# A decoder-layer kernel: rotary key tile in two weight passes, conditioning shared out anew between TensorE, GpSimd, VectorE and ScalarE

## The chip, the cores and the metric

The kernel runs on one core of a Trainium2 chip. Times are device microseconds of one launch, from the first to the last instruction of the core. Lower is better. TensorE multiplies, VectorE (DVE in the rows) and ScalarE (ACT) do the elementwise work out of SBUF and PSUM, GpSimd (POOL) does elementwise work out of SBUF alone, and SyncE (SP) issues most of the transfers.

## The reference

One hybrid decoder layer over 1024 tokens and 1024 features, in float32:

```python
mod = jax.nn.silu(c) @ w_ada[l] + b_ada[l]
shift, scale, gate = jnp.split(mod[:, None, :], 3, axis=-1)
h = rmsnorm(x, g_pre[l]) * (1.0 + scale) + shift
proj = h @ w_in[l]
(c_q, c_kv, k_pe, gate_mla, q_ret, k_ret, v_ret, gate_ret,
 merge_mla, merge_ret) = jnp.split(proj, pts, axis=-1)
y_mla = mla_branch(c_q, c_kv, k_pe, positions, g_q[l], w_q_up[l], g_kv[l], w_kv_up[l])
y_ret = retention_branch(q_ret, k_ret, v_ret, positions, g_ret[l]) * jax.nn.silu(gate_ret)
...
x = x + gate * (merged @ w_out[l])
return rmsnorm(x, g_final)
```

What matters here is the start. `c` is one vector of 1024 numbers; shift and scale are 2048 sums of 1024 products each ("the conditioning"). `h` is the normed input, scaled and shifted per feature. `k_pe` is 64 of the columns of `proj`; it is one rotary key shared by all eight heads, and inside `mla_branch` it is turned by the rotary angles, where component i and component i+32 are mixed.

## The kernel before, in words

**Precision.** Every float32 product is made of three passes over TensorE in the format fp32r: an operand is split into a rounded high part (`_hi`, written by ScalarE, `split_weight` for weights, `high` for h) and the remainder (`_lo`, written by VectorE, `lower_weight` and `low`), and the passes are hi·hi, hi·lo and lo·hi. `w_raw`, `w_hi` and `w_lo` are rings of three weight tiles of 128 columns.

**The start, in order.** x arrives, is normed on VectorE and turned on TensorE (`x_t`, features on partitions). The conditioning weights `ada` come in four quarters q, each with shift and scale for two feature tiles of h. In a quarter the 1024 inputs stand as eight tiles k of 128 partitions: GpSimd multiplies tile 0 by silu(c) (line 976, into `stage`), VectorE adds tiles 1 to 7 on (`weigh`, lines 1501 and 1508, into `ada_sum`), and TensorE then sums over the partitions with a column of ones (`weigh_sums`, line 1951). In quarter 0 TensorE multiplies tile 0 itself (line 1984), with silu(c) as the moving column. VectorE adds bias and gain (`modulation`, lines 1516 to 1521), and signals `mod_ready`.

**h.** From `mod`, ScalarE makes the rounded `h_hi` (line 1090) and GpSimd the full `h_full` (line 984), both 128x1024 for each feature tile; VectorE subtracts them into `h_lo` (line 1528). VectorE's queue for a quarter is: `weigh(q+1)`, `low(2q)`, `low(2q+1)`, `modulation(q+1)`.

**First three tiles.** r = 0 is the rotary key tile: its 128 columns are the 64 of `k_pe` twice. r = 1 and 2 are the first latent tiles. TensorE does them feature tile by feature tile as h comes: `early_hi` (lines 1968 and 1969: w_hi·h_hi and w_lo·h_hi for two halves of 512 tokens each) and `early_lo` (line 1976: w_hi·h_lo). In front of `early_lo(2q)` stands `weigh_sums(q+1)`. Feature tiles 6 and 7 are done tile by tile of r. Then r = 3, 4, 5 run in full (`products`, lines 2005 to 2007), 48 matmuls each.

**The rotary key and the sums of h.** After `low(7)` VectorE goes through: the MLA angles (`angles(1)`, lines 1445 to 1451), `lower_weight(3)`, the retention angles (`angles(0)`), `lower_weight(4)` and `(5)`; then k_pe times cosine (line 1554), the swapped halves times sine (1555), their sum (1558); then four sums or differences over parts of h (1561 to 1569), their low parts (1572), and the low part of the first "form" (1579), a combination of weights for the stage that follows: 25 pairs of weight tiles in a seven-product scheme (`pair_products`, lines 2090 to 2093). ScalarE meanwhile evicts `k_pe` from PSUM (line 1198), and SyncE copies it with its blocks of 32 rows swapped into `swap` (line 668), after VectorE's first instruction of the retention angles (`table` 8). GpSimd starts the sums of pair 0 when `roped` is 5.

Everything behind (the 25 pairs, up-projections, attention with the value projection filled in, retention, merge, output) is the same in both kernels.

Of the kernel before, what the change touches and what calls it, by code (L numbers as in the profile page):

```python
# [21 lines left out]
P = 128  # L22
# [87 lines left out]
ADA_STEPS = KD - 1  # L110
# [10 lines left out]
class Layer:  # L121
# [3 lines left out]
    def __init__(self, nc, sem, a, t, d, out, pools):  # L125
# [113 lines left out]
        self.out_stage = [self.stage[:, 0, :], self.stage[:, 1, :], late_stage[:, 0, :], late_stage[:, 1, :]]  # L239
        self.v_stage = [nc.alloc_sbuf_tensor_at("v_stage_0", [P, 2, HALF], F32R, offset=stage_at),  # L240
# [285 lines left out]
    def lower_weight(self, dve, r):  # L526
        if r >= R_END:
            return
        dve.wait_ge(*((self.w_hi_ready, r) if r else (self.first_w_hi_ready, 1)))
        self.nc.vector.tensor_tensor(self.lo_place(r), self.raw_place(r), self.hi_place(r).bitcast(F32), ALU.subtract)\  # L530
            .then_inc(self.w_lo_ready, 1)
# [88 lines left out]

    def form_bank(self, pair, n):

        return (5 * pair + n + 3) % 8
# [23 lines left out]
    def sync(self, sp):  # L647
# [26 lines left out]
        sp.wait_ge(self.roped, 5)  # L674
# [290 lines left out]
    def gpsimd(self, pool):  # L965
        nc, rot = self.nc, self.rot
        nc.gpsimd.memset(self.t["ones"][:, :], 1.0).then_inc(self.ones_ready, 1)

        def weigh(q):

            part = self.stage[:, q % 2, :].rearrange("p (s n) -> p s n", s=2)
            pool.wait_ge(self.ada_loaded[q], 16)
            if q >= 2:
                pool.wait_ge(self.ada_step, ADA_STEPS * (q - 1))
            pool.wait_ge(self.silu_ready, 1)
            nc.gpsimd.tensor_scalar(part, self.ada[:, q, :, 0, :], self.silu_c[:, 0:1], None, ALU.mult)                .then_inc(self.ada_part, 1)

        def full(k):
            c = 4 * (k // 2) + k % 2
            pool.wait_ge(self.mod_ready, 2 * (k // 2) + 2)  # L980
            if k == 0:
                pool.wait_ge(self.x_early, X_EARLY)
                pool.wait_ge(self.x_late, 2 * KD - X_EARLY)
            nc.gpsimd.tensor_scalar(self.h_tile(k), self.x_t[:, k, :], self.mod[:, c + 2:c + 3],
                                    self.mod[:, c:c + 1], ALU.mult, ALU.add).then_inc(self.h_full_ready, 1)

        for q in range(4):
            if q < 3:
                weigh(q + 1)
            full(2 * q)  # L990
            full(2 * q + 1)
        for pair in range(PAIRS):
            a11, a12, total, a21 = (self.form_source(FORMS * pair + n) for n in (0, 4, 1, 3))
            a22 = self.form_source(FORMS * pair + 5)
            made = SUMS + FORMS * pair
            pool.wait_ge(self.pair_loaded[pair % 2], 16 * (pair // 2 + 1))
            if pair:
                pool.wait_ge(self.form_lo, made - FORMS + 2)
            else:
                pool.wait_ge(self.roped, 5)  # L1000
# [59 lines left out]
    def scalar(self, act):  # L1060
# [31 lines left out]

        self.split_weight(act, 1)
# [4 lines left out]
        for k in range(1, KD):  # L1098
            high(k)
        for r in range(R_UP):  # L1100
# [375 lines left out]
    def vector(self, dve):  # L1476
# [16 lines left out]
        def weigh(q):  # L1493

            out = self.ada_sum[:, q, :, :]
            dve.wait_ge(self.ada_loaded[q], 16)
            dve.wait_ge(self.ada_part, q) if q else dve.wait_ge(self.silu_ready, 1)
            for k in range(1, KD):
                before = out
                if k == 1 and q == 0:  # L1500
                    nc.vector.tensor_scalar(out, self.ada[:, 0, :, 1, :], self.silu_c[:, 1:2], None, ALU.mult)\
                        .then_inc(self.ada_step, 1)
                    continue
                if k == 1:
                    before = self.stage[:, q % 2, :].rearrange("p (s n) -> p s n", s=2)
                else:
                    dve.wait_ge(self.ada_step, ADA_STEPS * q + k - 1)
# [24 lines left out]
        dve.wait_ge(self.w_loaded[0], 16)  # L1532
        nc.vector.tensor_copy(self.w_hi[:, 0, :], self.w_raw[:, 0, :]).then_inc(self.first_w_hi_ready, 1)
# [23 lines left out]
        dve.wait_ge(self.roped, 2)  # L1557
# [4 lines left out]
        dve.wait_ge(self.roped, 4)  # L1562
# [364 lines left out]
    def tensor(self, pe):  # L1927
# [18 lines left out]
        def weigh_sums(q):  # L1946
            pe.wait_ge(self.ada_step, ADA_STEPS * (q + 1))
# [11 lines left out]
        def early_hi(k, tiles):  # L1959

            pe.wait_ge(self.h_hi_ready, k + 1)
            for r in tiles:
                if k == 0:
                    pe.wait_ge(self.w_lo_ready, r + 1)
                for half in range(2):
# [3 lines left out]
                    nc.tensor.matmul(out, w_lo[:, r, cut], h_hi[:, k, tok], start=False, stop=False)  # L1969
# [599 lines left out]
```

## Time and profile before

| what | value |
|---|---|
| median of 3 runs | 1615.43 us |
| the runs | 1615.06, 1615.43, 1618.31 us |
| span of the profiled execution | 1616.2 us (the page gives no other time for it) |
| TensorE, busy share of the span | 97% |
| VectorE, ScalarE, GpSimd | 59%, 37%, 20% |
| mean granted TensorE clock | 0.994 of full |

The busy shares are means over stages with different limits. In a row of the timeline the columns are start, busy time, engine, line, operation, tiles and count, and in brackets the idle time in front of it and who ended it. Matmuls of 512 columns are pipelined, so a row shows 0.39 us where the next one starts 0.227 us later. A row that ends in x2 or more is several instructions merged.

### The profile page before, as it was taken

The numbers are of one execution on the slowest core, as the hardware profiler recorded it, in microseconds if no ns is written. First come the engines' busy times: TensorE is split into PE (matmuls) and PEld (weight loads), VectorE is DVE, ScalarE is ACT, GpSimd is POOL, SyncE is SP. The second block draws the span as 40 slices with busy tenths as digits, with TensorE's granted clock in tenths as the row PEclk, the third lists the DMA queues.
The fourth block names the chain that finished last, engine by engine and source line by source line (L and its number), as shares of the span: only waits on it lengthen the run. The fifth ranks groups of instructions, "written<-read, shape, count | busy, mean of one in ns | idle before, by whom it ended". The sixth has DMA issues, their size and how long they took to land. (4 is left out here: it accounts for less than half of the span.)

```text
span 1616.2 us, 20288 instructions
## 1 busy us (share of the span) xinstructions
PE 1568.4 (97%) x7568; PEld 1308.9 (81%) x7568; DVE 959.4 (59%) x1626; ACT 605.1 (37%) x1057; POOL 322.0 (20%) x280
## 2 busy tenths in 40 slices
PE   5999999999999999999999999899999999999998
PEld 4778888888888888798888888787688888888886
DVE  6984444444444457752566665567987775647544
ACT  5444333333333343342343433334544443213111
POOL 2232223322322200200000000015655530000000
PEclk9999999999999999999999999999999999999999
DMA  9132332223323334799265554447977767345422
GB/s 385 38 130 105 111 112 110 107 109 115 120 104 111 95 97 164 301 414 322 82 209 170 181 184 164 179 137 260 323 235 228 250 204 281 115 137 183 143 105 78
DMA packets 142225, 278.70 MB, mean 172 GB/s; under 512 B 11056, under 2 KB 83632, under 8 KB 133552
## 3 DMA queue, kind: packets, MB, share of 16 engines
q1 hardware_dynamic: 125488, 245.09, 43.6%
q10 hardware_dynamic: 12032, 15.54, 2.9%
q0 software_dynamic: 4608, 16.78, 2.7%
q8 instruction: 61, 1.00, 0.2%
q14 instruction: 36, 0.29, 0.1%
HBM read 182.47 MB, written 94.37 MB: 171 GB/s over the span
## 5 line engine op out<-in xcount | busy, mean ns | idle before, releaser
L1579 DVE TENSOR_TENSOR w_form<-w_pair,w_form 128x512 fp32r<-128x512 f32 x150 | 116.3, 776 | 127.2 <-ACT w_form L1211 125.6
L1211 ACT ACTIVATE w_form<-w_pair 128x512 fp32r<-128x512 f32 x150 | 94.6, 632 | 245.3 <-PE p_banks L2093 237.2
L2090 PE MATMUL p_banks<-h_hi,w_form 128*128 128x512 f32 x300 | 116.8, 389 | 1.1 <-DVE w_form L1579 1.1
L2093 PE MATMUL p_banks<-h_hi,w_form 128*128 128x512 f32 x300 | 116.7, 389 | 0.0
L2092 PE MATMUL p_banks<-h_lo,w_form 128*128 128x512 f32 x300 | 116.7, 389 | 0.0
L1283 ACT ACTIVATE prob<-p_banks,neg_max 128x128 f32<-128x128 f32 (+3 forms) x64 | 47.5, 742 | 182.9 <-DVE neg_max L1693 182.9
L524 ACT ACTIVATE w_hi<-w_raw 128x1024 fp32r<-128x1024 f32 (+2 forms) x69 | 59.5, 866 | 144.9 <-PE p_banks L2348 96.2
L2348 PE MATMUL p_banks<-y_hi,w_lo 128*128 128x512 f32 x256 | 99.6, 389 | 0.0
L2347 PE MATMUL p_banks<-y_lo,w_hi 128*128 128x512 f32 x256 | 99.6, 389 | 0.0
L2346 PE MATMUL p_banks<-y_hi,w_hi 128*128 128x512 f32 x256 | 99.6, 389 | 0.0
L1055 POOL DMA_DIRECT2D v_ret<-v_stage x32 | 17.7, 554 | 410.1 <-DVE v_stage L1670 410.0
L530 DVE TENSOR_TENSOR w_lo<-w_raw,w_hi 128x1024 fp32r<-128x1024 f32 (+3 forms) x70 | 72.0, 1033 | 35.4 <-ACT w_hi L524 34.7
L2132 PE MATMUL p_banks<-w_hi,h_hi 128*128 128x512 f32 x192 | 78.8, 410 | 0.6 <-DVE w_lo L530 0.6
L1008 POOL TENSOR_TENSOR w_pair<-w_pair 128x512 f32<-128x512 f32 x25 | 32.5, 1299 | 232.2 <-DVE w_form L1579 232.2
L2090 PE MATMUL p_banks<-h_sum_hi,w_form 128*128 128x512 f32 x200 | 77.9, 389 | 0.0
L2093 PE MATMUL p_banks<-h_sum_hi,w_form 128*128 128x512 f32 x200 | 77.8, 389 | 0.0
L2092 PE MATMUL p_banks<-h_sum_lo,w_form 128*128 128x512 f32 x200 | 77.8, 389 | 0.0
L2090 PE MATMUL p_banks<-h_forms,w_form 128*128 128x512 f32 x200 | 77.8, 389 | 0.0
L2092 PE MATMUL p_banks<-h_forms,w_form 128*128 128x512 f32 x200 | 77.8, 389 | 0.0
L2093 PE MATMUL p_banks<-h_forms,w_form 128*128 128x512 f32 x200 | 77.8, 389 | 0.0
L2132 PE MATMUL p_banks<-w_lo,h_hi 128*128 128x512 f32 x192 | 76.6, 399 | 0.0
L2132 PE MATMUL p_banks<-w_hi,h_lo 128*128 128x512 f32 x192 | 76.5, 398 | 0.0
(316 smaller groups left out, 4302.7 us busy)
## 6 DMA issues: line engine op xcount, KB each, us to landing
w_pair<-in_w_pairs SPq DMA_DIRECT2D x25, 1024.0 KB, 4.9
w_raw<-in_w_dense SPq DMA_DIRECT2D x45, 512.0 KB, 4.7
v_ret<-v_stage POOLq DMA_DIRECT2D x32, 512.0 KB, 3.4
v_chunk<-v_ret SPq DMA_DIRECT2D x32, 512.0 KB, 3.7
merge_t<-act_t SPq DMA_DIRECT2D x48, 256.0 KB, 3.4
act_t<-stage SPq DMA_DIRECT2D x40, 256.0 KB, 2.0
act_t<-stage_late SPq DMA_DIRECT2D x40, 256.0 KB, 2.0
ada<-in_w_ada SPq DMA_DIRECT2D x4, 2048.0 KB, 23.9
```

The source lines that it names most:

```text
L524: self.nc.scalar.activation(self.hi_place(r), self.raw_place(r), ACT.Copy).then_inc(self.w_hi_ready, 1)
L530: self.nc.vector.tensor_tensor(self.lo_place(r), self.raw_place(r), self.hi_place(r).bitcast(F32), ALU.subtract)\
L1211: self.nc.scalar.activation(self.form[f % FORM_SLOTS][:, 0, :], self.form_source(f), ACT.Copy).then_inc(self.form_hi, 1)
L1283: nc.scalar.activation(self.prob[:, g % 2, 0:width], p[:, 6:8, :].rearrange("p a n -> p (a n)")[:, 0:width], ACT.Exp, bias=self.neg_max[:, ...
L1579: nc.vector.tensor_tensor(self.form[f % FORM_SLOTS][:, 1, :], self.form_source(f), self.form[f % FORM_SLOTS][:, 0, :].bitcast(F32), ALU.su ...
L2090: self.nc.tensor.matmul(out, w_hi[:, cut], x_hi[:, q, :], start=fresh and q == 0, stop=False, skip_group_check=True)
L2092: self.nc.tensor.matmul(out, w_hi[:, cut], x_lo[:, q, :], start=False, stop=False, skip_group_check=True)
L2093: last = self.nc.tensor.matmul(out, w_lo[:, cut], x_hi[:, q, :], start=False, stop=q == KD // 2 - 1, skip_group_check=True)
L2132: ins = self.nc.tensor.matmul(self.p[:, FILL_BANKS[unit % 3], :], h[:, k, tok], w[:, cut], start=(k == 0 and kind == 0), stop=(k == KD - 1 ...
L2346: self.nc.tensor.matmul(out, self.w_hi[:, slot, cut], self.y_hi[y][:, tok], start=(k == 0), stop=False)
L2347: self.nc.tensor.matmul(out, self.w_hi[:, slot, cut], self.y_lo[y][:, tok], start=False, stop=False)
L2348: return self.nc.tensor.matmul(out, self.w_lo[:, slot, cut], self.y_hi[y][:, tok], start=False, stop=(k == KD - 1))
```

## The change

1. **Rotary key tile in two passes.** `lower_weight(0)` writes the low part of the 64 columns into the second 64 columns of `w_hi` of tile 0, instead of a `w_lo` tile. `early_hi` leaves out the w_lo pass for r = 0. Rows 0 to 63 of the product then hold hi·h, rows 64 to 127 lo·h. SyncE copies the halves, exchanged, into a new tile `k_other` (in the place of `stage`), and VectorE adds it to `k_pe` behind the retention angles. `roped` counts one more from there on.
2. **Conditioning.** In quarter 0 TensorE multiplies tiles 0, 1 and 2 (`PE_K`), VectorE 3 to 7. In quarters 1 to 3 GpSimd multiplies tiles 0 and 1 in place and adds them (`POOL_K`), VectorE takes 2 to 7.
3. **h_full** goes from GpSimd to ScalarE, behind both `high` of its quarter; the first `w_hi` goes from VectorE to ScalarE.

```diff
@@ lower_weight
+        if r == 0:
+            second, raw = (w.rearrange("p (k n) -> p k n", n=P)[:, :, ROPE:P] for w in (self.hi_place(0), self.raw_place(0)))
+            self.nc.vector.tensor_tensor(second, raw, second.bitcast(F32), ALU.subtract).then_inc(self.w_lo_ready, 1)
+            return
@@ sync
         sp.wait_ge(self.evicted, 2)
+        for half in range(2):
+            sp.dma_start(self.k_other[ROPE * half:ROPE * (half + 1), :], self.k_pe[ROPE * (1 - half):ROPE * (2 - half), :])\
+                .then_inc(self.swapped, 16)
         sp.wait_ge(self.table, 8)
+        sp.wait_ge(self.roped, 1)
         for q in range(4):
             sp.dma_start(self.swap[32 * q:32 * q + 32, :], self.k_pe[32 * (q ^ 1):32 * (q ^ 1) + 32, :])\
@@ gpsimd
+            for k, part in enumerate((first, second)):
+                nc.gpsimd.tensor_scalar(part, part, self.silu_c[:, k:k + 1], None, ALU.mult).then_inc(self.ada_part, 1)
+            pool.wait_ge(self.ada_part, 3 * q - 1)
+            nc.gpsimd.tensor_tensor(first, first, second, ALU.add).then_inc(self.ada_part, 1)
@@ scalar
+        def full(k):
+            c = 4 * (k // 2) + k % 2
+            nc.scalar.activation(self.h_tile(k), self.x_t[:, k, :], ACT.Identity,
+                                 scale=self.mod[:, c + 2:c + 3], bias=self.mod[:, c:c + 1]).then_inc(self.h_full_ready, 1)
+        act.wait_ge(self.w_loaded[0], 16)
+        nc.scalar.activation(self.w_hi[:, 0, :], self.w_raw[:, 0, :], ACT.Copy).then_inc(self.first_w_hi_ready, 1)
...
-        for k in range(1, KD):
+        high(1)
+        full(0)
+        full(1)
+        for k in range(2, KD, 2):
             high(k)
+            high(k + 1)
+            full(k)
+            full(k + 1)
@@ vector
         weigh(0)
-        dve.wait_ge(self.w_loaded[0], 16)
-        nc.vector.tensor_copy(self.w_hi[:, 0, :], self.w_raw[:, 0, :]).then_inc(self.first_w_hi_ready, 1)
         modulation(0)
...
             if r == RING:
                 self.angles(dve, 0)
+                dve.wait_ge(self.swapped, 32)
+                nc.vector.tensor_tensor(self.k_pe[:, :], self.k_pe[:, :], self.k_other[:, :], ALU.add).then_inc(self.roped, 1)
         dve.wait_ge(self.sines, 2)
-        dve.wait_ge(self.swapped, 64)
+        dve.wait_ge(self.swapped, 96)
@@ tensor
                     nc.tensor.matmul(out, w_hi[:, r, cut], h_hi[:, k, tok], start=(k == 0), stop=False)
-                    nc.tensor.matmul(out, w_lo[:, r, cut], h_hi[:, k, tok], start=False, stop=False)
+                    if r:
+                        nc.tensor.matmul(out, w_lo[:, r, cut], h_hi[:, k, tok], start=False, stop=False)
...
-            nc.tensor.matmul(p[:, 6, 16 + c:17 + c], self.ada[:, 0, c // 2, 0, c % 2 * P:(c % 2 + 1) * P],
-                             self.silu_c[:, 0:1], start=True, stop=True)
+            for k in range(PE_K):
+                nc.tensor.matmul(p[:, 6, 16 + c:17 + c], self.ada[:, 0, c // 2, k, c % 2 * P:(c % 2 + 1) * P],
+                                 self.silu_c[:, k:k + 1], start=(k == 0), stop=(k == PE_K - 1))
```

VectorE's queue from the end of the MLA angles to the first sum over h, before:

```order
L1451 TENSOR_SCALAR angle_mla<-angle_mla 128x1024
L530 TENSOR_TENSOR w_lo<-w_raw,w_hi 128x1024
L1445 TENSOR_SCALAR angle_ret<-positions,consts 128x1024
L1446 TENSOR_SCALAR turns_ret<-angle_ret 128x1024
L1447 TENSOR_SCALAR turns_ret<-turns_ret 128x1024
L1449 SCALAR_TENSOR_TENSOR angle_ret<-turns_ret,angle_ret 128x1024 x3
L1451 TENSOR_SCALAR angle_ret<-angle_ret 128x1024
L530 TENSOR_TENSOR w_lo<-w_raw,w_hi 128x1024 x2
L1554 TENSOR_TENSOR k_pe<-k_pe,cos_mla 128x1024
```

The same stretch of VectorE's queue in the changed kernel:

```order
L1461 TENSOR_SCALAR angle_ret<-positions,consts 128x1024
L1462 TENSOR_SCALAR turns_ret<-angle_ret 128x1024
L1463 TENSOR_SCALAR turns_ret<-turns_ret 128x1024
L1465 SCALAR_TENSOR_TENSOR angle_ret<-turns_ret,angle_ret 128x1024 x3
L1467 TENSOR_SCALAR angle_ret<-angle_ret 128x1024
L1568 TENSOR_TENSOR k_pe<-k_pe,k_pe_other_half 128x1024
L536 TENSOR_TENSOR w_lo<-w_raw,w_hi 128x1024 x2
L1571 TENSOR_TENSOR k_pe<-k_pe,cos_mla 128x1024
```

The addition of the exchanged halves stands between the retention angles and the two low parts of weights.

ScalarE's queue in the conditioning, from the end of the copies of `x_t` to the eviction of the rotary key tile, before:

```order
L524 ACTIVATE w_hi<-w_raw 128x1024
L1090 ACTIVATE h_hi<-x_t,mod 128x1024
L524 ACTIVATE w_hi<-w_raw 128x1024
L1090 ACTIVATE h_hi<-x_t,mod 128x1024 x7
L1198 ACTIVATE k_pe<-p_banks 128x512 x2
```

And in the changed kernel:

```order
L1102 ACTIVATE w_hi<-w_raw 128x1024
L526 ACTIVATE w_hi<-w_raw 128x1024
L1093 ACTIVATE h_hi<-x_t,mod 128x1024
L526 ACTIVATE w_hi<-w_raw 128x1024
L1093 ACTIVATE h_hi<-x_t,mod 128x1024
L1098 ACTIVATE h_full<-x_t,mod 128x1024 x2
L1093 ACTIVATE h_hi<-x_t,mod 128x1024 x2
L1098 ACTIVATE h_full<-x_t,mod 128x1024 x2
```

ScalarE now makes two full tiles behind two rounded ones in each quarter.

## Rows read from the trace of the kernel before

**Rows 1.** The page, section 1: busy time of each engine

```profile
PE 1568.4 (97%) x7568; PEld 1308.9 (81%) x7568; DVE 959.4 (59%) x1626; ACT 605.1 (37%) x1057; POOL 322.0 (20%) x280
```

**Rows 2.** Timeline, TensorE at the two hand-overs behind the first tiles

```profile
74.23 0.50 PE L2005 MATMUL p_banks<-h_hi,w_hi 128*128 128x512 f32 x1 [1.55 <-DVE w_lo L530]
...
106.77 0.39 PE L2007 MATMUL p_banks<-h_hi,w_lo 128*128 128x512 f32 x1
108.28 0.50 PE L2090 MATMUL p_banks<-h_hi,w_form 128*128 128x512 f32 x1 [1.12 <-DVE w_form L1579]
```

**Rows 3.** Timeline, VectorE from the MLA angles to the first form

```profile
66.33 0.75 DVE L1445 TENSOR_SCALAR angle_mla<-positions,consts 128x1024 f32<-128x1024 int32 x1
...
72.95 1.22 DVE L530 TENSOR_TENSOR w_lo<-w_raw,w_hi 128x1024 fp32r<-128x1024 f32 x1
74.09 0.75 DVE L1445 TENSOR_SCALAR angle_ret<-positions,consts 128x1024 f32<-128x1024 int32 x1
...
80.72 2.35 DVE L530 TENSOR_TENSOR w_lo<-w_raw,w_hi 128x1024 fp32r<-128x1024 f32 x2
82.99 1.22 DVE L1554 TENSOR_TENSOR k_pe<-k_pe,cos_mla 128x1024 f32<-128x1024 f32 x1
...
107.55 0.68 DVE L1579 TENSOR_TENSOR w_form<-w_pair,w_form 128x512 fp32r<-128x512 f32 x1
```

**Rows 4.** The tile k_pe_swap: SyncE's four copies, and their landing

```profile
L668 SPq DMA_DIRECT2D k_pe_swap<-k_pe x4: 582/594/618, 74.9 to 76.8; - x4
...
DMA to landing us min/median/max: 2.3/2.3/2.4
```

**Rows 5.** Timeline, VectorE: single operations of the conditioning, alone and beside GpSimd

```profile
32.82 0.75 DVE L1508 SCALAR_TENSOR_TENSOR ada_sum<-ada,silu_c,stage 128x512 f32<-128x512 f32 x1
42.49 1.59 DVE L1508 SCALAR_TENSOR_TENSOR ada_sum<-ada,silu_c,ada_sum 128x512 f32<-128x512 f32 x1
49.08 2.36 DVE L1528 TENSOR_TENSOR h_lo<-h_full,h_hi 128x1024 fp32r<-128x1024 f32 x2
61.47 0.16 DVE L1521 SCALAR_TENSOR_TENSOR mod<-mod,cols 128x2 f32<-128x2 f32 x1
```

**Rows 6.** Timeline, GpSimd: products of the conditioning, full tiles of h, a sum

```profile
27.26 1.63 POOL L976 TENSOR_SCALAR stage<-ada,silu_c 128x512 f32<-128x512 f32 x1 [26.44 <-DMA ada<-in_w_ada]
34.45 1.98 POOL L976 TENSOR_SCALAR stage<-ada,silu_c 128x512 f32<-128x512 f32 x1
61.73 1.20 POOL L984 TENSOR_SCALAR h_full<-x_t,mod 128x1024 f32<-128x1024 f32 x1 [7.11 <-DVE mod L1521]
90.15 3.21 POOL L1001 TENSOR_TENSOR w_sum<-w_pair 128x512 f32<-128x512 f32 x1 [25.00 <-DVE k_rope_made L1563]
...
115.17 1.28 POOL L1001 TENSOR_TENSOR w_sum<-w_pair 128x512 f32<-128x512 f32 x1
```

**Rows 7.** The tile ada: its transfers' landing in us from issue

```profile
L656 SPq DMA_DIRECT2D ada<-in_w_ada x4: 436/895/1202, 4.1 to 8.5; - x4
...
DMA to landing us min/median/max: 16.9/23.9/30.5
```

**Rows 8.** Timeline, TensorE and ScalarE in the conditioning: partition sums, products, h_hi

```profile
26.91 1.05 PE L1951 MATMUL p_banks<-ones,ada_sum 128*128 128x1 f32 x8 [2.37 <-DVE ada_sum L1508]
...
43.29 0.39 PE L1968 MATMUL p_banks<-h_hi,w_hi 128*128 128x512 f32 x1
43.52 0.39 PE L1969 MATMUL p_banks<-h_hi,w_lo 128*128 128x512 f32 x1
...
61.67 2.38 ACT L1090 ACTIVATE h_hi<-x_t,mod 128x1024 fp32r<-128x1024 f32 x2 [7.55 <-DVE mod L1521]
```

**Rows 9.** Windows: busy time of each engine, then granted TensorE clock, DMA share, GB/s

```profile
24.50:26.90 2.40, 0.04 (x1) 0.00 (x0) 2.30 (x4) 0.98 (x2) 0.00 (x0) 1.00 0.91 377
26.90:28.00 1.10, 1.05 (x8) 0.97 (x8) 0.56 (x2) 0.00 (x0) 0.74 (x1) 1.00 1.24 518
28.00:30.10 2.10, 0.00 (x0) 0.00 (x0) 2.03 (x5) 1.43 (x2) 2.10 (x2) 0.75 1.04 445
30.10:34.00 3.90, 3.83 (x9) 3.12 (x10) 3.80 (x4) 1.89 (x2) 3.90 (x2) 0.50 0.98 416
35.80:38.40 2.60, 2.60 (x12) 1.89 (x10) 2.49 (x4) 0.00 (x0) 0.63 (x1) 0.99 0.93 371
```

More of the change, by code:

```diff
@@ L109 @@
 X_EARLY, X_BANKS = 5, [0, 1, 2, 3, 4, 5, 7]
-ADA_STEPS = KD - 1
+POOL_K = 2
+PE_K = 3
 CHUNKS = [1, 1, 1, 1, 2, 2, 2, 2]
@@ L239, in __init__ @@
         self.out_stage = [self.stage[:, 0, :], self.stage[:, 1, :], late_stage[:, 0, :], late_stage[:, 1, :]]
+        self.k_other = nc.alloc_sbuf_tensor_at("k_pe_other_half", [P, S], F32, offset=stage_at)
         self.v_stage = [nc.alloc_sbuf_tensor_at("v_stage_0", [P, 2, HALF], F32R, offset=stage_at),
@@ L619, in v_stores, with ada_steps @@
         return sum(self.v_slot(n) == self.v_slot(unit) for n in range(unit))
+    def ada_steps(self, q):
+        return KD - PE_K + (KD - POOL_K) * (q - 1) if q else 0
     def form_bank(self, pair, n):
@@ L673, in sync @@
         sp.dma_start(d["ret_tables"].rearrange("a p n -> p a n"), self.ret_made[:, :, :]).then_inc(self.tables_stored, 16)
-        sp.wait_ge(self.roped, 5)
+        sp.wait_ge(self.roped, 6)
         sp.dma_start(d["k_rope"], self.k_rope_made[:, :, :].bitcast(F32)).then_inc(self.tables_stored, 16)
@@ L969, in weigh @@
         def weigh(q):
-            part = self.stage[:, q % 2, :].rearrange("p (s n) -> p s n", s=2)
+            first, second = (self.ada[:, q, :, k, :] for k in range(POOL_K))
             pool.wait_ge(self.ada_loaded[q], 16)
-            if q >= 2:
-                pool.wait_ge(self.ada_step, ADA_STEPS * (q - 1))
             pool.wait_ge(self.silu_ready, 1)
[L976 to L991, printed above, removed]
+            for k, part in enumerate((first, second)):
+                nc.gpsimd.tensor_scalar(part, part, self.silu_c[:, k:k + 1], None, ALU.mult).then_inc(self.ada_part, 1)
+            pool.wait_ge(self.ada_part, 3 * q - 1)
+            nc.gpsimd.tensor_tensor(first, first, second, ALU.add).then_inc(self.ada_part, 1)
+        for q in range(1, 4):
+            weigh(q)
         for pair in range(PAIRS):
@@ L999, in gpsimd @@
             else:
-                pool.wait_ge(self.roped, 5)
+                pool.wait_ge(self.roped, 6)
             nc.gpsimd.tensor_tensor(total, a21, a22, ALU.add).then_inc(self.form_sums, 1)
@@ L1106, in scalar @@
                 self.sines_of(act, 0)
-                act.wait_ge(self.roped, 3)
+                act.wait_ge(self.roped, 4)
                 nc.scalar.activation(self.k_rope_made[:, 0, :], self.k_pe[:, :], ACT.Copy).then_inc(self.roped, 1)
@@ L1495, in weigh @@
             out = self.ada_sum[:, q, :, :]
+            first = POOL_K if q else PE_K
             dve.wait_ge(self.ada_loaded[q], 16)
-            dve.wait_ge(self.ada_part, q) if q else dve.wait_ge(self.silu_ready, 1)
-            for k in range(1, KD):
+            dve.wait_ge(self.ada_part, 3 * q) if q else dve.wait_ge(self.silu_ready, 1)
+            for k in range(first, KD):
                 before = out
-                if k == 1 and q == 0:
-                    nc.vector.tensor_scalar(out, self.ada[:, 0, :, 1, :], self.silu_c[:, 1:2], None, ALU.mult)\
+                if k == first and q == 0:
+                    nc.vector.tensor_scalar(out, self.ada[:, 0, :, k, :], self.silu_c[:, k:k + 1], None, ALU.mult)\
                         .then_inc(self.ada_step, 1)
                     continue
-                if k == 1:
-                    before = self.stage[:, q % 2, :].rearrange("p (s n) -> p s n", s=2)
+                if k == first:
+                    before = self.ada[:, q, :, 0, :]
                 else:
-                    dve.wait_ge(self.ada_step, ADA_STEPS * q + k - 1)
+                    dve.wait_ge(self.ada_step, self.ada_steps(q) + k - first)
                 nc.vector.scalar_tensor_tensor(out=out, in0=self.ada[:, q, :, k, :], scalar=self.silu_c[:, k:k + 1],
@@ L1556, in vector @@
                                        in1=self.sin_mla[:, :], op0=ALU.mult, op1=ALU.mult).then_inc(self.roped, 1)
-        dve.wait_ge(self.roped, 2)
+        dve.wait_ge(self.roped, 3)
         nc.vector.tensor_tensor(self.k_pe[:, :], self.k_pe[:, :], self.swap[:, :], ALU.add).then_inc(self.roped, 1)
@@ L1561, in vector @@
         nc.vector.tensor_tensor(self.h_sum[0], h[:, :, 0, 1, :], h[:, :, 0, 0, :], ALU.subtract).then_inc(self.pair_done, 1)
-        dve.wait_ge(self.roped, 4)
+        dve.wait_ge(self.roped, 5)
         nc.vector.tensor_tensor(self.k_rope_made[:, 1, :], self.k_pe[:, :], self.k_rope_made[:, 0, :].bitcast(F32),
@@ L1946, in weigh_sums @@
         def weigh_sums(q):
-            pe.wait_ge(self.ada_step, ADA_STEPS * (q + 1))
+            pe.wait_ge(self.ada_step, self.ada_steps(q + 1))
             if q:
```

## The prediction

> **What bounds the kernel now.** I read the page's busy times first: TensorE works 97% of the span [rows 1], so a saving counts only if TensorE's own queue gets shorter at a place where it doesn't wait, or if what it waits for comes earlier. The change touches only the first 108 us. So I read the timeline of each engine there, and looked for TensorE's waits. Behind the first three tiles there are two [rows 2]: 1.55 us at 74.23 for the low part of weight tile 3, and 1.12 us at 108.28 for the first form. Both are ended by VectorE. VectorE's rows then show why [rows 3]: from 66.33 (the MLA angles) to the first form at 107.55 its operations stand end to end. This **VectorE chain** sets when the pair stage starts, and with it the end. TensorE's time ahead of it is covered: it stops at 107.16 (106.77 and 0.39) and waits.
>
> So the question is when the chain starts and how long it gets. The 16 matmuls that the two-pass tile saves (8 feature tiles, 2 halves), 0.227 us each by the distance of two starts [rows 8] or 3.6 us in all, are worth nothing by themselves: with them gone TensorE waits longer at 108.
>
> **The chain gets longer by 3.35 us.** Part one is the new addition of the exchanged halves, 128x1024, two inputs. The same kind of operation takes 1.22 us, and two in a row 2.27 from start to start [rows 3], so 1.15. Part two is a wait. Before, SyncE copies the swapped blocks from 74.9 on, at the first retention-angle operation; the last of four copies starts at 76.8 and lands 2.3 us later [rows 4], 79.1, well ahead of 82.99 where VectorE wants it [rows 3]: hidden. Now SyncE waits for the addition. Counted from the start of the chain (66.33 before): the retention angles end at 14.4 (80.72 less 66.33), the addition at 15.6, SyncE's fourth copy starts three spacings of 0.63 later, with 0.1 for the signal at 17.6, and lands at 19.9. VectorE has the low parts of tiles 4 and 5 to do meanwhile, 2.27 us [rows 3], and is through at 17.8. It stands for 2.2 us, and the product with the cosine starts at 20.0 instead of 16.65. Behind it nothing changes: the sums over h, GpSimd's sums of pair 0 (they wait for the rotary key as before), ScalarE's rounding. Queued behind SyncE's new wait are the load of pair 0 and two stores; pair 0 (issued at 82.0) has until GpSimd's 90.15 [rows 6], and it keeps its distance to the chain. The first two copies (k_other) are issued when ScalarE has evicted tile 0, over 10 us before the addition, hidden.
>
> **The chain starts 1.6 us earlier.** Quarter by quarter:
> - Quarter 0: TensorE's 8 more small products run behind the transposes, up to where VectorE, with two operations fewer, would have been; partition sums start up to 0.8 us before the 26.91 of [rows 8]. That gain ends at the next wait, for data.
> - Quarter 1: its weights land at about 27.2, when GpSimd starts [rows 6]. GpSimd now has three operations, not one. A product took 1.63 and, beside VectorE's two-input work, 1.98 us [rows 6]; a sum 1.28 alone and 3.21 beside such work [rows 6]. So 27.3 + 1.6 + 1.7 + 2 = about 32.7, and VectorE starts on quarter 1 where it does today (32.82 [rows 5]). It has one operation fewer, 0.79, but GpSimd now works all through it (quarter 2, landed at about 33, halfway between 27.2 and the 39.0 of quarter 3 below, takes 2 + 2 + 2 to 3 us), and an operation that takes 0.75 alone took 1.59 with GpSimd beside it; six of them took 6.6 us (42.49 to 49.08) where six alone are 4.7 [rows 5]. I take no gain here, 39.2 as now; bounds 36.6 (GpSimd in nobody's way) and 40.3.
> - Quarter 2: VectorE again has six operations, the first few beside GpSimd (quarter 3 lands at 8.5 + 30.5 = 39.0 [rows 7] and keeps GpSimd until 45 or later), about 6 us; TensorE needs h_hi (1.35 us) and 20 matmuls, 4.54, so 5.95. Both end at about 48.7 where VectorE now ends at 49.1, also with 0.5 us lost to GpSimd in the two h_lo ahead. Gain 0.4.
> - From there to the chain it took 17.2 us (49.1 to 66.33). Now: h_lo twice and modulation, 2.6; h_hi, 20 matmuls, partition sums 1.05 and modulation, 7.4; then ScalarE alone makes h_hi and h_full. Two h_hi take 2.38 from 61.67 on [rows 8], so four take 4.7, and h_lo of tile 7 behind them 1.2, together 6.0. Sum 16.0: gain 1.2. The last step itself is a loss: from the modulation at 61.63 (61.47 and 0.16 [rows 5]) to the chain it took 4.7 us, with GpSimd and ScalarE side by side.
>
> So the first form comes 3.35 - 1.6 = **1.75 us later**.
>
> **The clock.** TensorE's wait at the pair stage grows from 1.12 to 1.12 + 3.35 = 4.5 us, whatever the start of the chain, since its three tiles hang on it as well. Of such waits the trace has one near relative. In 24.5 to 30.1 TensorE was idle but for 1.05 us of one-column products; the granted clock fell from 1.00 to half (1.2 GHz) within 28.0 to 30.1, and it was half until 35.8 [rows 9], 5.7 us of matmuls at half speed, or 2.85 lost. After the waits of 1.55 and 1.12 us it stayed at 2.4 GHz. A wait of 4.5 is longer than the idle piece that led to the fall, and behind it the pairs start at once with dense work. I expect a fall, and a cost between 0 and 2.9, taken at 2.1, nearer to the one row there is.
> The Trainium skill (TensorE: Matmul & The Clock Gate, Part 1, the HAM clock gate) says that the clock falls to 1.2 GHz after idling and rises only after sustained work. By that the 2.1 us are due; the trace agrees for 28 to 36 us, and can't show it for this wait.
>
> **Sum**: 1.75 + 2.1 = 3.85 us. The page gives the profiled execution's span, 1616.2, and nothing around it; the median of the runs shown is 0.8 lower. On the median: 1615.4 + 3.85 = **1619.3 us**.
>
> **GpSimd's price is the weakest term.**
> The Trainium skill (GPSIMD Engine Reference, "When to use GPSIMD") has one-input elementwise work on GpSimd at roughly line rate; at the 1.2 GHz of that page 512 elements would be an estimated 0.43 us, where the rows show 1.63 and 1.98.
> Rows point the same way in one place: 1024 elements with multiply and add took 1.20 us when VectorE stood still [rows 6].
>
> **The rivals.**
> - **The chain is late, the clock stays.** Only 1.75 us: 1617.2. For it: the fall on record had a long thin stretch, not one wait. Against: its pieces were 2.4 and 2.1 us, half of 4.5.
> - **GpSimd is cheap.** At 0.6 a product (half of 1.20) and 1.28 a sum it needs 2.5 us a quarter. Quarter 1 then runs from 31.6 to 36.6, 2.6 earlier; quarter 2 is bound by TensorE, ends at 45.2; the chain starts at 61.2, 5.1 early. First form: 3.35 - 5.1 = -1.75; with the clock's 2.1 +0.35, without it -1.75: 1613.7 to 1615.8. For it: VectorE stands for short times only, so GpSimd's long rows may be VectorE's doing. Against: the 1.63 at 27.26, when VectorE did little.
> - **Faster.** The same, and the swapped copies are there when VectorE comes: -1.75 - 2.2 = -3.95, 1611.5, the clock untouched. It takes a landing within 0.1 us of issue where the rows say 2.3 [rows 4], or a chain start 2.2 us earlier still; from 3.2 us below it counts as faster.
> - **No gain in the conditioning.** GpSimd slows VectorE so much that the chain starts where it does: 3.35 + 2.1 = 5.45, 1620.9.
>
> **How the numbers follow.** This kernel's measurement tells about 0.2%, 3.2 us, from no change. Forecast case (late chain, clock falls): 0.52, from +2.2 to +5.6, of it 0.42 above 3.2. Clock stays: 0.18, same. GpSimd cheap: 0.16, same. Faster: 0.08. No gain: 0.06, slower. Together slower 0.48, same 0.44, faster 0.08. The range reaches down to the third case (1613.7) and up to the forecast's upper bound and the fourth case: 1613.8 to 1621.2.
>
> **What would show it.** TensorE's wait at its first form near 4.5 us, VectorE idle 2.2 us in front of the cosine product and released by the swap copies; the first h_lo of quarter 3 waiting for ScalarE; GpSimd's products near 2 us; matmuls of the first forms 0.43 us apart. The prediction is wrong if VectorE isn't idle there, if GpSimd's quarters take under 3 us, or if something of the pair stage waits for the load of pair 0.

## The result, and the profile after

| | before | the change |
|---|---|---|
| median of 20 runs each, taken side by side | 1616.74 us | 1621.30 us |
| lowest, highest | 1614.07, 1623.08 | 1616.79, 1626.00 |
| span of the profiled execution | 1616.2 us | 1618.5 us |
| time of that execution | not given | 1620.47 us |
| mean granted TensorE clock in it | 0.994 | 0.989 |

The ratio to the kernel before is 1.0020, 95% interval 1.0011 to 1.0029: slower by 1.8 to 4.7 us (the two medians differ by 4.56). The forecast was slower by 3.85. Its 1619.3 is 2.0 us under the median, of which 1.3 come from the kernel before: the three runs shown had a median of 1615.43, all twenty 1616.74.

The answers to [rows 2, 3] in the changed kernel. TensorE, timeline (start, busy time, engine, line, operation, tiles; idle time ahead and who ended it):

```profile
105.02 0.39 PE L2026 MATMUL p_banks<-h_hi,w_lo 128*128 128x512 f32 x1
109.86 0.79 PE L2109 MATMUL p_banks<-h_hi,w_form 128*128 128x512 f32 x1 [4.45 <-DVE w_form L1596]
110.45 0.63 PE L2111 MATMUL p_banks<-h_lo,w_form 128*128 128x512 f32 x1
```

VectorE, timeline, from the last modulation to the first form:

```profile
58.56 0.16 DVE L1538 SCALAR_TENSOR_TENSOR mod<-mod,cols 128x2 f32<-128x2 f32 x1
62.30 2.36 DVE L1545 TENSOR_TENSOR h_lo<-h_full,h_hi 128x1024 fp32r<-128x1024 f32 x2 [3.58 <-ACT h_full L1098]
64.58 0.75 DVE L1461 TENSOR_SCALAR angle_mla<-positions,consts 128x1024 f32<-128x1024 int32 x1
...
78.97 1.22 DVE L1568 TENSOR_TENSOR k_pe<-k_pe,k_pe_other_half 128x1024 f32<-128x1024 f32 x1
80.10 2.35 DVE L536 TENSOR_TENSOR w_lo<-w_raw,w_hi 128x1024 fp32r<-128x1024 f32 x2
84.57 1.23 DVE L1571 TENSOR_TENSOR k_pe<-k_pe,cos_mla 128x1024 f32<-128x1024 f32 x1 [2.12 <-DMA k_pe_swap<-k_pe]
...
109.12 0.68 DVE L1596 TENSOR_TENSOR w_form<-w_pair,w_form 128x512 fp32r<-128x512 f32 x1
```

The chain starts 1.75 us earlier (64.58, 66.33 before), and from its start to TensorE's first form it takes 45.28 us where it took 41.95. The added operation and the wait for the swapped copies stand in it by name. The first form comes 1.58 us late, and TensorE waits 4.45 us ahead of it, not 1.12. Behind the wait the clock is at half, by windows (busy time of PE, PEld, DVE, ACT, POOL, then granted clock, DMA share, GB/s):

```profile
76.00:103.00 27.00, 27.00 (x121) 22.35 (x120) 24.71 (x16) 14.62 (x13) 6.51 (x2) 1.00 0.54 175
108.00:112.00 4.00, 2.14 (x5) 1.76 (x6) 2.40 (x3) 0.43 (x1) 1.59 (x1) 0.63 0.00 0
112.00:116.00 4.00, 4.00 (x11) 3.07 (x11) 1.99 (x3) 2.83 (x6) 0.84 (x1) 0.51 0.00 0
116.00:120.00 4.00, 4.00 (x19) 3.33 (x18) 1.73 (x2) 1.13 (x3) 3.38 (x3) 1.00 0.00 0
```

**A marker for everything behind.** In the pair stage all engines run in step with TensorE, 19.04 us a pair. GpSimd's last sum of a pair shows the step. The row of the same pair, before, then in the change:

```profile
129.41 1.28 POOL L1008 TENSOR_TENSOR w_pair<-w_pair 128x512 f32<-128x512 f32 x1 [9.28 <-DVE w_form L1579]
```

```profile
133.54 1.29 POOL L1011 TENSOR_TENSOR w_pair<-w_pair 128x512 f32<-128x512 f32 x1 [9.53 <-DVE w_form L1596]
```

It is 21.13 us behind the first form before, 23.68 in the change. So the change costs 1.58 us on the chain and 2.55 by the clock, 4.13 at this point. Laid over each other, the two traces stay 4.1 us apart, matmul for matmul, from the marker to 700 us. The two spans differ by only 2.3, since the clock also falls in later stages, and not at the same places: in the trace of the kernel before it was half (0.50) from 1040 to 1046, where the change's was full, and between 1030 and 1046 the distance falls from 5.9 to 1.7. The marker is free of that, and the experiments are read by it (the expectations call it the metronome); times and ratios stand beside it. It has a limit: it is read from one execution a kernel, and a fall ahead of it can differ from one execution to the next.

### The profile page after: what moved, and what is told of

Read it like the earlier page. It is cut to its first block and busy times, and to the rows that moved or that the text cites. A ratio compares the mean times of both kernels' runs of the same rounds, so it can differ in the third digit from the quotient of the medians.

```text
span 1618.5 us, 20291 instructions
## 1 busy us (share of the span) xinstructions
PE 1570.0 (97%) x7568; PEld 1311.2 (81%) x7568; DVE 953.3 (59%) x1621; ACT 615.3 (38%) x1066; POOL 319.3 (20%) x278
## 5 line engine op out<-in xcount | busy, mean ns | idle before, releaser
L536 DVE TENSOR_TENSOR w_lo<-w_raw,w_hi 128x1024 fp32r<-128x1024 f32 (+2 forms) x69 | 70.0, 1018 | 34.7 <-ACT w_hi L526 34.1
```

## The experiments

Each ratio is to the kernel before, run on the same chip in the same rounds, from 5 to 12 executions of each kernel (20 of the change). "Chain" is the time from the MLA angles on VectorE to TensorE's first form, "lag" the time from that form to the marker.

| kernel | chain start | chain | TensorE's wait | lag | marker | ratio, 95% interval |
|---|---|---|---|---|---|---|
| before | 66.33 | 41.95 | 1.12 | 21.13 | 129.41 | 1 |
| the change | 64.58 | 45.28 | 4.45 | 23.68 | 133.54 | 1.0020, 1.0011 to 1.0029 |
| two_pass_only | 65.45 | 45.29 | 4.45 | 23.24 | 133.98 | 1.0029, 1.0017 to 1.0042 |
| conditioning_only | 66.40 | 41.94 | 1.06 | 21.13 | 129.47 | 0.9995, 0.9984 to 1.0006 |
| early_add | 66.17 | 43.08 | 2.24 | 21.09 | 130.34 | 1.0001, 0.9991 to 1.0012 |
| filled_wait | 63.25 | 45.29 | 0.83 | 21.11 | 129.65 | 1.0002, 0.9991 to 1.0014 |
| before_longer_chain | 66.43 | 45.60 | 4.75 | 23.68 | 135.71 | 1.0043, 1.0028 to 1.0059 |
| last_full_on_gpsimd | 63.37 | 45.30 | 4.42 | 22.20 | 130.87 | 1.0033, 1.0020 to 1.0046 |
| early_add_and_gpsimd | 63.70 | 43.08 | 2.24 | 22.35 | 129.13 | 1.0004, 0.9994 to 1.0014 |
| one_product_on_gpsimd | 61.92 | 45.29 | 4.45 | 23.12 | 130.33 | 1.0010, 0.9997 to 1.0024 |
| three_repairs | 61.45 | 43.08 | 2.24 | 21.12 | 125.65 | 0.9980, 0.9968 to 0.9991 |
| three_repairs_kept_warm | 60.12 | 43.08 | 0.65 | 21.12 | 124.32 | 0.9980, 0.9971 to 0.9990 |
| repairs_three_passes | 63.41 | 41.93 | 1.06 | 21.13 | 126.47 | 0.9984, 0.9972 to 0.9995 |

### The change in two halves

**two_pass_only** is the kernel before with part 1 of the change (`lower_weight(0)`, the exchanged halves, the addition, the counts), nothing of parts 2 and 3.

> The two-pass rotary tile alone, conditioning as before. My theory (the VectorE chain bounds, its length grows by the addition and the wait for the swapped copies, and the longer wait of TensorE costs clock): the chain starts at 66.0 to 66.4 (66.33 before), VectorE is idle about 2.2 us in front of the cosine product, the first form comes about 3.3 us later than before (111.3 to 111.7), TensorE waits 4.4 to 4.6 us there, the clock falls to half behind it. The metronome of the pair stage (GpSimd's last sum of the first pair that repeats, at 129.41 before and 133.54 in the change) comes at 135 to 136, and the median 5 to 7 us above the kernel before. Rival (16 matmuls fewer are 3.6 us fewer): the metronome 3 us or more ahead of 129.4.

The chain is 45.29 us long, the wait 4.45, the clock falls, ratio 1.0029. The marker, 133.98, and the median, 3.9 us above the kernel before, are lower than expected (135 to 136, and 5 to 7). The chain starts at 65.45, 0.9 earlier than before. The modulation of quarter 0 gives 0.3 of that, and the low part of tile 0, which is half as wide, 0.55: from that modulation to quarter 1 VectorE needs 3.80 us (28.17 to 31.97), not 4.35. TensorE's 16 saved matmuls bring nothing, as the wait shows:

```profile
110.74 0.79 PE L2102 MATMUL p_banks<-h_hi,w_form 128*128 128x512 f32 x1 [4.45 <-DVE w_form L1590]
```

**conditioning_only** is the change without part 1:

```diff
-                    if r:
-                        nc.tensor.matmul(out, w_lo[:, r, cut], h_hi[:, k, tok], start=False, stop=False)
+                    nc.tensor.matmul(out, w_lo[:, r, cut], h_hi[:, k, tok], start=False, stop=False)
...
-                dve.wait_ge(self.swapped, 32)
-                nc.vector.tensor_tensor(self.k_pe[:, :], self.k_pe[:, :], self.k_other[:, :], ALU.add).then_inc(self.roped, 1)
```

> The conditioning and the moved full tiles of h alone; rotary tile with three passes, no exchanged halves. My theory: VectorE's chain keeps its old length (41.9 us from the MLA angles to TensorE's first form), TensorE's wait stays at 1.1 us, the clock doesn't fall there. With 24 instead of 20 matmuls a quarter TensorE bounds the quarters, so the chain starts at 65.5 to 66.3, not at 64.6; the metronome at 128.6 to 129.4, the time 0 to 1 us below the kernel before. Rival (the conditioning itself makes the kernel slower): chain start later than 66.5 and a metronome behind 130.

Marker 129.47, 0.06 from before: the new sharing of the conditioning by itself is worth nothing, since with 24 matmuls a quarter TensorE bounds it. From modulation to modulation its last quarter takes 9.11 us, against 8.20 in the change with 20. The loss belongs to the two-pass tile. The chain start of 66.40 lies 0.1 beyond what was expected (65.5 to 66.3), and the marker 0.07. The last quarter shows the bound: VectorE waits there for TensorE's partition sums.

```profile
60.18 0.16 DVE L1527 TENSOR_TENSOR mod<-p_banks,cols 128x4 f32<-128x4 f32 x1 [1.88 <-PE p_banks L1957]
66.40 0.75 DVE L1452 TENSOR_SCALAR angle_mla<-positions,consts 128x1024 f32<-128x1024 int32 x1
```

### The wait for the swapped copies

```diff
             if r == RING:
-                self.angles(dve, 0)
                 dve.wait_ge(self.swapped, 32)
                 nc.vector.tensor_tensor(self.k_pe[:, :], self.k_pe[:, :], self.k_other[:, :], ALU.add).then_inc(self.roped, 1)
+                self.angles(dve, 0)
```

> The change, with the addition of the exchanged halves ahead of the retention angles instead of behind them, so that the swapped copies land under VectorE's work. My theory: chain start 64.6 as in the change, no idle time in front of the cosine product, first form at 107.6 to 107.8 (109.85 in the change), TensorE's wait 2.3 us instead of 4.4. If the clock fall hangs on the length of that wait it may stay away: metronome at 128.5 to 129; if it falls all the same, 131 to 131.6. Median 2 to 5 us below the change. Rival (something else in the chain takes the place of the copies, for instance the load of pair 0): first form stays at 109 or later.

The idle time in front of the cosine product is gone, and the chain is 43.08 us long, 2.20 less. TensorE's wait is 2.24 and no fall follows (lag 21.09). Rows of VectorE, then TensorE:

```profile
73.93 1.22 DVE L1567 TENSOR_TENSOR k_pe<-k_pe,k_pe_other_half 128x1024 f32<-128x1024 f32 x1
...
83.97 1.22 DVE L1571 TENSOR_TENSOR k_pe<-k_pe,cos_mla 128x1024 f32<-128x1024 f32 x1
```

```profile
109.25 0.50 PE L2109 MATMUL p_banks<-h_hi,w_form 128*128 128x512 f32 x1 [2.24 <-DVE w_form L1596]
```

What missed is the chain start: 66.17, not 64.6, and with it the first form (109.25) and the marker (130.34). The first form is even where the rival wanted it, at 109 or later, but not for the rival's reason: nothing took the place of the copies in the chain. In this execution the clock fell inside the conditioning, as in the change's own, and longer:

```profile
39.00:42.00 3.00, 1.85 (x8) 1.48 (x8) 2.97 (x5) 0.00 (x0) 3.00 (x2) 0.64 1.04 407
42.00:46.00 4.00, 4.00 (x11) 3.12 (x10) 3.86 (x6) 3.89 (x4) 3.92 (x3) 0.50 0.18 72
46.00:50.00 4.00, 4.00 (x17) 3.24 (x17) 3.96 (x4) 0.75 (x1) 0.55 (x1) 0.91 0.00 0
```

### The clock behind the long wait

**filled_wait** puts work without a use into the wait:

```diff
+        for n in range(16):
+            nc.tensor.matmul(p[:, 7, :], h_hi[:, 0, 0:P], h_hi[:, 0, 0:HALF], start=True, stop=True)
         for pair in range(PAIRS):
             self.pair_products(pe, pair)
```

> The change, with 16 matmuls of 512 columns between weight tile 5 and the first form whose result nobody reads (bank 7 is overwritten later); 3.6 us of work inside a wait of 4.4. If the clock is what costs behind the wait: first form at 109.85 as in the change, granted clock 1.00 behind it, metronome at 130.5 to 131 instead of 133.54, median 2 to 3 us below the change. Rival (the clock isn't what costs there, or falls for another reason): metronome stays at 133.5.

```profile
103.92 3.79 PE L2036 MATMUL p_banks<-h_hi 128*128 128x512 f32 x16
108.54 0.50 PE L2111 MATMUL p_banks<-h_hi,w_form 128*128 128x512 f32 x1 [0.83 <-DVE w_form L1596]
```

```profile
108.50:112.00 3.50, 3.46 (x14) 2.63 (x15) 1.27 (x2) 1.74 (x4) 1.60 (x1) 1.00 0.00 0
```

The chain is unchanged, 45.29, and so is the time at which TensorE can begin relative to it; the lag is 21.11 where the change has 23.68. So the clock, and not something in the pairs, costs the 2.57 us. The first form and the marker came 1.3 and 0.9 to 1.3 us ahead of what was expected, since here the clock didn't fall a second time in the conditioning. In the times the ratios of this kernel (up to 1.0014) and of the change (from 1.0011) just overlap.

**before_longer_chain** goes the other way: nothing of the change, only a longer chain.

```diff
+        for n in range(3):
+            if n:
+                dve.wait_ge(self.table, 14 + n)
+            nc.vector.tensor_tensor(self.k_other[:, :], self.h_tile(0), self.h_tile(1), ALU.add).then_inc(self.table, 1)
         dve.wait_ge(self.sines, 2)
         dve.wait_ge(self.swapped, 64)
```

> The kernel before with nothing of the change, but three more 128x1024 additions on VectorE (into unused space) in front of the cosine product: the chain longer by the 3.35 us that the change adds to it. My theory: first form 3.3 to 3.5 us later relative to the chain start (45.3 us after it), TensorE's wait 4.4 to 4.6 us, granted clock 0.5 behind it for 6 us or more, and the metronome 23.2 to 23.7 us behind the first form where it is 21.1 without a fall: 134 to 136 with a chain start at 66.3. Rival (the fall belongs to something else in the change, not to the wait): the metronome 21.1 us behind the first form.

The chain got 3.65 us longer (the three wait for each other), and the kernel before shows all of it: wait 4.75, lag 23.68, ratio 1.0043. A chain longer by 3.65 us moves the marker by 6.3.

```profile
112.03 0.79 PE L2095 MATMUL p_banks<-h_hi,w_form 128*128 128x512 f32 x1 [4.75 <-DVE w_form L1584]
```

```profile
135.71 1.29 POOL L1009 TENSOR_TENSOR w_pair<-w_pair 128x512 f32<-128x512 f32 x1 [9.53 <-DVE w_form L1584]
```

### The start of the chain

**last_full_on_gpsimd**: in `scalar`, `full(k)` and `full(k + 1)` only for k < 6; in `gpsimd`, behind the three `weigh`:

```diff
+        full(6)
+        full(7)
```

> The change, with the two full tiles of h of the last quarter made by GpSimd again, beside ScalarE's two rounded ones. My theory: the chain starts 3.5 to 4.0 us behind the last modulation instead of 6.0, so 61.0 to 62.5 where the change has 64.58 (if the clock in the conditioning is alike); its length stays 45.3, TensorE's wait 4.4, the clock falls behind it; metronome 130.5 to 132. Rival (the order on ScalarE costs nothing): chain start 6 us behind the modulation as before the edit.

From the last modulation to the chain it took 4.86 us, against 6.02 in the change: better by 1.16, not by the 2 to 2.5 that were expected, and the chain starts at 63.37, not at 61.0 to 62.5. VectorE still waits twice for GpSimd, as in the kernel before:

```profile
58.51 0.16 DVE L1547 SCALAR_TENSOR_TENSOR mod<-mod,cols 128x2 f32<-128x2 f32 x1
60.05 1.23 DVE L1554 TENSOR_TENSOR h_lo<-h_full,h_hi 128x1024 fp32r<-128x1024 f32 x1 [1.38 <-POOL h_full L996]
62.23 1.23 DVE L1554 TENSOR_TENSOR h_lo<-h_full,h_hi 128x1024 fp32r<-128x1024 f32 x1 [0.94 <-POOL h_full L996]
```

The second full tile takes GpSimd 2.2 us beside VectorE's two-input subtraction, where the first took 1.2. The ratio, 1.0033, isn't told apart from that of the change. Here the marker and the time disagree: the marker is 1.46 us behind the kernel before, the six executions are slower by 3.2 to 7.4 us. The traced one had a short fall behind the 4.42 us wait, half clock from 108.1 to 111.5, where the change had it from 109.1 to 116; what the others had isn't known.

> Both repairs: the addition of the halves ahead of the retention angles, the last two full tiles on GpSimd. My theory: chain start 61 to 63, chain 43.1 us long, TensorE's wait 2.2 us, no clock fall behind it, metronome 125.5 to 127.5 (129.41 before): 2 to 4 us faster than the kernel before. It fails if a clock fall in the conditioning moves the chain start behind 63.5.

**early_add_and_gpsimd** has both edits. The chain starts at 63.70 and misses the 63.5 that the expectation set as its limit, again with a fall in the conditioning; and here the clock fell behind the 2.24 us wait too (lag 22.35, against 21.09 in early_add). The ratio is 1.0004: it only gives back the loss.

**one_product_on_gpsimd** takes GpSimd's second product and sum back:

```diff
-            for k, part in enumerate((first, second)):
-                nc.gpsimd.tensor_scalar(part, part, self.silu_c[:, k:k + 1], None, ALU.mult).then_inc(self.ada_part, 1)
-            pool.wait_ge(self.ada_part, 3 * q - 1)
-            nc.gpsimd.tensor_tensor(first, first, second, ALU.add).then_inc(self.ada_part, 1)
+            nc.gpsimd.tensor_scalar(first, first, self.silu_c[:, 0:1], None, ALU.mult).then_inc(self.ada_part, 1)
```

with `POOL_K = 1` and the wait of VectorE on `q` instead of `3 * q`.

> The change, with GpSimd making one product a quarter as before and VectorE adding seven tiles, not six: it prices the second product and the sum on GpSimd. My theory (what VectorE saves in quarter 1 it loses to waiting for GpSimd and to GpSimd beside it): VectorE ends quarter 1 at 37.5 to 38.5 as in the change (37.8); in quarters 2 and 3 it takes 0.8 us more work, less the shorter time beside GpSimd; chain start within 0.7 us of the change. Rival (GpSimd's share is what makes the conditioning faster): quarter 1 ends at 39 or later and the chain starts 2 us later.

My own theory missed too, on the low side. VectorE ended quarter 1 at 37.29, with one operation more, half a microsecond ahead of the change (37.82); its two h_lo took 2.35 us, not 3.42; and the chain started at 61.92, 2.66 us earlier. The second product on GpSimd is worse than nothing for the start of the chain. The change's GpSimd and VectorE in quarter 1:

```profile
27.09 3.86 POOL L989 TENSOR_SCALAR ada<-ada,silu_c 128x512 f32<-128x512 f32 x2 [26.27 <-DMA ada<-in_w_ada]
31.03 1.45 POOL L991 TENSOR_TENSOR ada<-ada 128x512 f32<-128x512 f32 x1
```

```profile
32.60 0.75 DVE L1525 SCALAR_TENSOR_TENSOR ada_sum<-ada,silu_c 128x512 f32<-128x512 f32 x1 [1.25 <-POOL ada L991]
...
37.82 3.42 DVE L1545 TENSOR_TENSOR h_lo<-h_full,h_hi 128x1024 fp32r<-128x1024 f32 x2
```

And VectorE with one product on GpSimd:

```profile
37.29 2.35 DVE L1542 TENSOR_TENSOR h_lo<-h_full,h_hi 128x1024 fp32r<-128x1024 f32 x2
```

Part of the 2.66 us is the clock: in this execution it didn't fall around quarter 1's partition sums, as in filled_wait, whose chain started at 63.25 with GpSimd's full share. (It fell later, at 60.8, too late to move VectorE.) Against filled_wait the second product and the sum cost 1.3 us. In the time that isn't shown: the ratio, 1.0010, is told apart neither from the change's nor from 1.

### A version that beats both

**three_repairs** is the change with the three edits above: one product on GpSimd, the last two full tiles on GpSimd, the addition ahead of the retention angles.

> The change with three repairs: one product a quarter on GpSimd (VectorE adds seven tiles), the last two full tiles of h on GpSimd, the addition of the halves ahead of the retention angles. From the single edits: chain start 61.9 less 1.1 = 60.8, chain 43.1 us, first form at 103.9, TensorE's wait 2.2 us. Without a clock fall behind that wait (the addition's own run had none, the run with two repairs had one) the metronome comes at 125.0, with one at 126 to 127.6; 129.41 before. Median 2 to 4.5 us below the kernel before. It fails if the fixed part behind the pair stage takes the gain back.

Marker 125.65, median 1613.50 against 1616.69 of the kernel before, ratio 0.9980 (0.9968 to 0.9991): faster than before by 1.5 to 5.2 us. Against the change no ratio was measured in one set of runs; the intervals to the kernel before don't overlap (1.0011 to 1.0029). The marker is in GpSimd's row:

```profile
125.65 1.29 POOL L1016 TENSOR_TENSOR w_pair<-w_pair 128x512 f32<-128x512 f32 x1 [9.22 <-DVE w_form L1602]
```

The chain started 0.65 us later than expected. In this execution the clock was half from 25.7 on, ahead of the partition sums of quarter 0, whose modulation came at 28.62 (27.47 in the change).

**three_repairs_kept_warm** adds 5 matmuls without a use in front of the partition sums of quarter 1 and 7 in front of the pairs.

> The same with idle waits of TensorE partly filled by matmuls that nobody reads: 5 in front of the partition sums of quarter 1 (1.4 us of wait), 7 in front of the first form (2.2 us of wait). First form at 103.9 to 104.2, granted clock 1.00 behind it, metronome 125.0 to 125.3; median 4 to 5 us below the kernel before, and at or below the kernel without the fillers by 0 to 2 us.

The marker is the earliest of all, 124.32, but that isn't the work of the fillers as far as the traces show. The lag is 21.12 with them and without them, since three_repairs had no fall behind its 2.24 us wait either. The 1.33 us were there before the first filler could act: quarter 0's modulation came at 27.09 here, at 28.62 there. In the time the two aren't told apart: 1613.70 and 1613.50, the same ratio. That these fillers are worth anything is not shown.

**repairs_three_passes** has the repaired conditioning with the rotary tile in three passes, as before (the addition and the copies fall away).

> The conditioning and its repairs (one product on GpSimd, last full tiles on GpSimd) with the rotary tile in three passes as before: it tells what the two-pass tile is worth once the rest is mended. TensorE then has 24 matmuls in a quarter, 0.9 us more, and bounds the quarters, so the chain starts about 2 us later than with two passes, at 62.5 to 63.5; the chain is 41.95 us long, the first form comes at 104.5 to 105.5, TensorE's wait 1.1 us, no clock fall behind it, metronome 125.6 to 126.6. Median 2.5 to 4 us below the kernel before. If it comes at or below the kernel with two passes, the two-pass tile isn't worth its addition.

Chain start 63.41, chain 41.93, marker 126.47, ratio 0.9984. Of the gain of three_repairs, 3.76 us at the marker, the conditioning gives 2.94 with three passes, and the two-pass tile adds 0.8, which the times (1613.86 and 1613.50) don't tell apart. The marker of this one has a fall in the conditioning in it (half clock from 38.7 to 42.1), so even the 0.8 isn't certain.

## Why the prediction was right

The mechanism held: a longer chain, and a fall of the clock behind the longer wait. That the start of the chain came within 0.15 us of the forecast was in part luck. Point by point, by its own steps:

- **The bound**: VectorE's chain from the MLA angles to the first form. Right. Five kernels with the late swap have 45.28 to 45.30 us, whatever else they do, and the pair stage starts with it. before_longer_chain shows it from the other side.
- **The chain gets longer by 3.35**: measured 3.33. The wait for the copies, put at 2.2, was 2.12, and early_add took 2.20 out of the chain by moving one instruction. The landing of 2.3 us from issue [rows 4] held for all four copies.
- **The chain starts 1.6 earlier**: measured 1.75. The total was right, but several of its parts were not, and they met by luck.
  - Quarter 1: VectorE began quarter 1 at 32.60 (32.7 by the working), but GpSimd's two products took 3.86 us where 3.3 were counted, and its sum 1.45 where 2 were. GpSimd beside VectorE was priced too high: VectorE's six operations took 5.2 us, not 6.6, so quarter 1 ended 1.3 us sooner (37.82 for 39.16) where no gain was taken.
  - Quarter 2: against that the two h_lo beside GpSimd took 3.42 us, 1.07 more than alone, priced at 0.5. Quarter 2 ended 1.6 us sooner (47.46 for 49.08), where 0.4 was taken (the working's own terms, 39.2, 2.5, 0.5 and 6, make 48.2 and not its 48.7).
  - Behind it: the surplus of 1.2 was lost to a fall of the clock in quarter 2 that isn't in the working at all. The fall made TensorE late, and VectorE waited for its partition sums twice, by 0.34 and 0.97 us. From the end of quarter 2 to the modulation it took 3.06 us where 2.6 were counted, the next quarter 8.20 where 7.4 were; filled_wait, without this fall, has 2.62 and 7.41. The last step took 5.86, 6.0 by the working. Modulations of the change, then the first of them in filled_wait:

```profile
50.16 0.16 DVE L1536 TENSOR_TENSOR mod<-p_banks,cols 128x4 f32<-128x4 f32 x1 [0.34 <-PE p_banks L1968]
58.37 0.16 DVE L1536 TENSOR_TENSOR mod<-p_banks,cols 128x4 f32<-128x4 f32 x1 [0.97 <-PE p_banks L1968]
```

```profile
49.63 0.15 DVE L1536 TENSOR_TENSOR mod<-p_banks,cols 128x4 f32<-128x4 f32 x1
```

- **The clock**: the wait was put at 4.5 (4.45) and the fall at 2.1 of a possible 2.9. The five kernels with a wait of 4.4 to 4.8 us show 1.1 to 2.55 by the lag; the change's execution has 2.55, so the term was 0.45 too small for it, and inside its bounds. That it falls there was an inference from one stretch with other work in it; filled_wait and before_longer_chain make it a finding.
The Trainium skill (TensorE: Matmul & The Clock Gate, Part 1) has the clock fall after idling and rise after sustained work. The trace agrees, in rows 105.02 to 110.45 above and in the windows behind.
- **The rivals.** "The clock stays" didn't come. "GpSimd is cheap" is refuted: its products took 1.56 to 3.58 us each where 0.6 was the condition, and taking one away made the conditioning faster. "Faster" and "no gain in the conditioning" didn't come either: the copies landed 2.3 us after issue, and the chain started 1.75 earlier. Two slips in the rivals' working (31.6 and 4.7 make 36.3 and not 36.6; the copies would have had 0.2 us and not 0.1) change no outcome.
The Trainium skill (GPSIMD Engine Reference, "When to use GPSIMD") has one-input work there at roughly line rate, an estimated 0.43 us for 512 elements. No row here shows it: the shortest product took 1.56 us, and VectorE was seldom still beside it.
- **Where the text fell short**: it says that the 16 matmuls "are worth nothing by themselves". With the old conditioning that holds (two_pass_only, where VectorE never waited for the partition sums of quarters 1 to 3). With the new one they shorten the quarters: with 20 the chain of the change starts at 64.58, with 24 that of conditioning_only at 66.40, and the last quarter, 8.20 against 9.11 us, shows four matmuls of 0.227. The working of quarter 2 used the 20, so the sum had it; the sentence didn't.

## What to carry to other kernels

A saving on the engine with the highest busy share is worth only what the wait behind it leaves; find the chain that ends that wait, and count what the edit adds to it, with the transfer that has to be issued anew because its source is now ready later. Place a step that a transfer waits for ahead of long work of the same engine, not behind it: here one line moved was 2.2 us. Ask of every TensorE wait that an edit makes longer whether the clock comes back at full speed. Price the work that is given to GpSimd beside a VectorE that is the bound: here taking back one product and one sum a quarter started the chain 1.3 us earlier. And compare early stages over more than one execution, since here a fall of the clock moved the same instructions as far as the edits did.

## What the runs showed of the hardware that was not expected

- The clock falls in the conditioning too. In the change TensorE waits 1.60 and 1.15 us around 37 to 40 with little work between, and the windows show half speed behind it:

```profile
36.00:38.00 2.00, 0.40 (x3) 0.05 (x1) 1.93 (x4) 0.00 (x0) 1.92 (x2) 1.00 0.94 383
38.00:41.00 3.00, 1.85 (x11) 1.66 (x12) 3.00 (x2) 0.00 (x0) 3.00 (x2) 0.97 1.07 386
41.00:44.30 3.30, 3.30 (x9) 2.52 (x9) 3.17 (x6) 2.54 (x3) 3.30 (x2) 0.51 0.51 201
```

  filled_wait runs the same program up to there, and in its execution the clock stayed: the chain started at 63.25, not 64.58. At the end of quarter 2 the two were only 0.1 us apart, so the same instructions end about 1.2 us apart by this fall alone; early_add's, with the longest fall, started at 66.17.
- Behind the same wait the clock falls in one execution and not in another. Behind 2.24 us at the pairs: no fall in early_add and three_repairs, one in early_add_and_gpsimd, which cost 1.2 us at the marker. Behind 1.91 us for the h_lo of feature tile 6: one in the change (half clock from 64.7 to 68.1), none in filled_wait and early_add. That one cost the chain nothing, since VectorE was past it.
- GpSimd and VectorE slow each other: the change's GpSimd took 5.60 us for the two products of quarter 3 and 3.57 for those of quarter 2; VectorE's two h_lo took 3.42 beside it and 2.35 without.
- Left open: how often each fall comes over many executions. One trace per kernel shows single cases, and the spread of the runs (about 9 us between lowest and highest) is wider than all effects here.
